# Forty modulation sums go from the expert stage to the first mixer branch, and ScalarE weighs the column one-hots of the gate stage

## The chip, the core and the metric

The kernel runs on one core of a Trainium2 chip. The metric is the device time of one execution in microseconds; less is better. The engines of the core are named as in the profile: PE (TensorE, the matmuls), PEld (its weight loads), DVE (VectorE), ACT (ScalarE), POOL (GpSimd) and SP (SyncE, which here only issues DMAs).

## The reference, cut to what matters

Two transformer-like blocks run one after the other on 512 tokens of width 1024. The first ends in a product-key expert layer ("PEER"), and this is where most of the change lies:

```python
def peer(h, wq, k1, k2, u, v):
    q = (tok @ wq).reshape(-1, PEER_HEADS, 2, PEER_SUB_DIM)
    s1 = einsum("nhd,kd->nhk", q[:, :, 0], k1); s2 = einsum("nhd,kd->nhk", q[:, :, 1], k2)
    v1, i1 = top_k(s1, 16); v2, i2 = top_k(s2, 16)
    cand = v1[..., :, None] + v2[..., None, :]
    top_s, top_c = top_k(cand, 16)               # 16 experts for each of 8 heads
    expert = i1[top_c // 16] * 128 + i2[top_c % 16]
    gate = softmax(top_s)
    act = gelu(einsum("pd,ped->pe", x, u[expert]))
    out = einsum("pe,ped->pd", gate * act, v[expert])
```

Every token picks 128 of 16384 experts. The second block needs modulation values, `silu(c) @ w + b`: each column is a sum over 1024 products. They depend on the input `c` alone, so they can be computed at any time before the second block.

## The kernel before

The program is a row of phases: front, the first mixer branch (`hgrn`, eight heads), the second branch (`gla`, four heads), `mix_out`, `peer`, an attention layer, a dense layer, a scan layer and a last dense layer. Every large product is done as three matmuls of fp32r parts: ACT copies a weight tile of 128x1024 into its high part (`high`), POOL or DVE subtracts that from the tile to get the low part, and PE multiplies.

In `peer`, 384 tokens are computed densely. PE multiplies them with all 128 tiles of `u` (an "up" tile, `up(n)`, 24 matmuls); ACT applies Gelu, and the result is stored to memory (`acts`). Afterwards PE multiplies with all 128 tiles of `v` (the expert stage, last part). What a token gives to an expert is weighted by its gate, which is zero for experts that it did not pick. The table of gates is built on PE in the gate stage: 48 groups of eight tokens, `gate(g)`. For a group DVE writes two sets of one-hots, the rows (which first key, `h` in the profile's names, because they lie in that memory) and the columns (which second key, `peer_cols`), and the columns are multiplied with the gate value. PE multiplies columns by rows for each of the eight tokens, and ACT copies the result from PSUM into `peer_slab`, in two pieces. Rows and columns have two buffers each, so DVE can be two groups ahead.

The order of the work is written out by hand. Each of three blocks has sixteen groups. After a group comes one up tile, except where `g % 5 == 4`: after groups 4, 9 and 14 the next group follows at once. After the sixteen groups come `TAILS` of 7, 8 and 3 up tiles. On ACT a group is `gate(g)` (two copies) and then `up(n)` (Gelu, then `high` of the tile two places on). After the first and the second block ACT also starts the stores of the table to memory.

The other 128 tokens (`FEW`) are handled one expert slot at a time on DVE: POOL fetches the picked rows of `u` with an indirect DMA (`fetch(e)`, eight slots), and DVE multiplies and sums a row of 1024 (`few`, L2049). 128 such row products must be done before the Gelu of these tokens. `MID` and `END` say how many stand in a head of the routing (the top-16 searches of DVE, before the gate stage), `few_after` and `TAIL_FEW` how many stand in the gate stage.

The routing ends when DVE has normalized the gates (L2101). PE then transposes them (L1829), does one more up tile and starts the groups.

The modulation sums are `M.dot` (L192): a DVE instruction over 128x1024 with an accumulated sum. 40 of them stand in the last part of `peer`, with a POOL queue that loads their tiles of 512 KB; the remaining 56 stand in a later dense phase. There `M.rows` is `silu(c)`, computed by ACT and POOL at the start of that part.

## Time and profile before

| | |
|---|---|
| median of three runs | 3612.22 us (3612.14 to 3612.56) |
| profiled execution | 3614.4 us, of which the span from first to last instruction is 3612.7 us |
| mean granted PE clock | 0.975 of full speed |
| PE busy | 3392.0 us (94%) |
| DVE busy | 2415.6 us (67%) |
| ACT busy | 1494.8 us (41%) |
| POOL busy | 1116.7 us (31%) |
| DMA | 604.52 MB |

PE works nearly all the time, so a change moves the end where it removes or adds a wait of PE, or a stretch at a lower PE clock. The busy time of the other engines matters only where PE waits for them. The profile counts each fp32 matmul of the gate products twice (sixteen for a group of eight tokens).

### The profile page before, as it was taken

Reading aid. Unit: us, or ns where it says so; the run is one execution under the profiler, and the core shown is the slowest. Engines: PE = TensorE matmul, PEld = TensorE weight load, DVE = VectorE, ACT = ScalarE, POOL = GpSimd, SP = SyncE. Lnnn points to the kernel's source line nnn. Section 1 sums busy time; section 2 is a strip of 40 time slices with the busy share of each in tenths; the row PEclk is TensorE's granted clock in tenths of the full one; section 3 lists DMA queues with packets and bytes.
Section 4 is the critical chain, followed back from the end, with each engine's and each line's share of the span. In section 5 each row is a group of like instructions: output and inputs, shape, how many; then the busy total and the mean of one; then the engine's idle time right before and its main releaser. Section 6 shows DMA issues by size and latency. Waiting matters only on the chain. (4 is left out here: it accounts for less than half of the span.)

```text
span 3612.7 us, 46897 instructions
## 1 busy us (share of the span) xinstructions
PE 3392.0 (94%) x17929; PEld 2997.4 (83%) x17929; DVE 2415.6 (67%) x4185; ACT 1494.8 (41%) x2094; POOL 1116.7 (31%) x741
## 2 busy tenths in 40 slices
PE   7999989979989999899999999989899998799998
PEld 6888867768879999789999999977688877678886
DVE  6555534435637799978679999766588776755354
ACT  5555545435443333445433333355432234343222
POOL 1222212207326777566543333110200025220002
PEclk9999999989999999899999999999999999899999
DMA  5111111116526777688799999830276522223331
GB/s 189 56 50 57 40 41 47 41 37 228 179 95 190 232 245 257 207 348 296 263 341 373 372 375 376 301 102 18 69 239 223 176 80 58 57 76 100 99 98 61
DMA packets 229823, 604.52 MB, mean 167 GB/s; under 512 B 27840, under 2 KB 102848, under 8 KB 228192
## 3 DMA queue, kind: packets, MB, share of 16 engines
q1 hardware_dynamic: 179696, 409.42, 34.3%
q0 software_dynamic: 47552, 173.04, 12.9%
q10 hardware_dynamic: 2352, 19.07, 1.3%
q8 instruction: 143, 2.34, 0.3%
q14 instruction: 80, 0.66, 0.1%
HBM read 550.31 MB, written 46.14 MB: 165 GB/s over the span
## 5 line engine op out<-in xcount | busy, mean ns | idle before, releaser
L1398 PE MATMUL peer_banks<-peer_h_parts,peer_w_parts 128*128 128x384 f32 (+1 forms) x3456 | 653.0, 348 | 31.6 <-POOL peer_w_parts L1709 26.5
L1398 PEld LDWEIGHTS peer_banks<-peer_h_parts,peer_w_parts 128*128 128x128 f32 x3456 | 611.8, 191 | 58.6 <-POOL peer_w_parts L1709 35.4
L1398 PE MATMUL peer_banks<-peer_act_parts,peer_w_parts 128*128 128x384 f32 x3072 | 535.4, 335 | 4.1 <-DVE peer_w_parts L2153 2.1
L1398 PEld LDWEIGHTS peer_banks<-peer_act_parts,peer_w_parts 128*128 128x128 f32 x3072 | 533.7, 188 | 5.0 <-DVE peer_w_parts L2153 4.7
L1398 PE MATMUL ffn_ps<-h_parts,ffn_w_parts 128*128 128x512 f32 x1920 | 441.0, 392 | 18.2 <-DVE h_parts L2837 11.0
L1398 PEld LDWEIGHTS ffn_ps<-h_parts,ffn_w_parts 128*128 128x128 f32 x1920 | 362.8, 189 | 94.9 <-DVE ffn_w_parts L2647 15.5
L1398 PE MATMUL ffn_ps<-ffn_hidden,ffn_w_parts 128*128 128x512 f32 x1920 | 438.1, 390 | 1.5 <-DVE ffn_hidden L2744 1.5
L1709 POOL TENSOR_TENSOR peer_w_parts<-slots,peer_w_parts 128x1024 fp32r<-128x1024 f32 x142 | 347.9, 2451 | 263.7 <-ACT peer_w_parts L1882 263.4
L1398 PEld LDWEIGHTS ffn_ps<-ffn_hidden,ffn_w_parts 128*128 128x128 f32 x1920 | 360.3, 188 | 77.7 <-issue 3.1
L1882 ACT ACTIVATE peer_w_parts<-slots 128x1024 fp32r<-128x1024 f32 x272 | 287.2, 1056 | 327.5 <-PE peer_banks L1398 311.5
L2492 ACT ACTIVATE ffn_w_parts<-slots 128x1024 fp32r<-128x1024 f32 x160 | 168.6, 1056 | 325.2 <-PE ffn_ps L1398 276.9
L2647 DVE TENSOR_TENSOR ffn_w_parts<-slots,ffn_w_parts 128x1024 fp32r<-128x1024 f32 x160 | 197.7, 1239 | 128.0 <-ACT ffn_w_parts L2492 127.7
L1398 PE MATMUL heads_proj_ps<-h_parts,hgrn_w_parts 128*128 128x512 f32 x960 | 269.4, 413 | 9.2 <-DVE hgrn_w_parts L1054 8.6
L1896 ACT ACTIVATE h<-peer_banks 128x384 f32<-128x384 f32 x128 | 63.0, 492 | 393.8 <-PE peer_banks L1398 380.5
L2153 DVE TENSOR_TENSOR peer_w_parts<-slots,peer_w_parts 128x1024 fp32r<-128x1024 f32 x128 | 156.5, 1223 | 67.3 <-ACT peer_w_parts L1882 67.2
L1398 PEld LDWEIGHTS heads_proj_ps<-h_parts,hgrn_w_parts 128*128 128x128 f32 x960 | 168.2, 190 | 39.9 <-DVE hgrn_w_parts L1054 8.7
L528 POOL TENSOR_TENSOR hgrn_w_parts<-x,hgrn_w_parts 128x1024 fp32r<-128x1024 f32 x38 | 96.2, 2532 | 291.0 <-ACT hgrn_w_parts L764 291.0
L1398 PE MATMUL heads_proj_ps<-h_parts,gla_w_parts 128*128 128x512 f32 x576 | 168.1, 430 | 8.9 <-POOL gla_w_parts L528 5.1
L1398 PEld LDWEIGHTS heads_proj_ps<-h_parts,gla_w_parts 128*128 128x128 f32 x576 | 108.6, 199 | 33.3 <-POOL gla_w_parts L528 7.7
L1322 DVE TENSOR_TENSOR mix_out_w_parts<-out_slots,mix_out_w_parts 128x1024 fp32r<-128x1024 f32 x40 | 80.3, 2007 | 81.0 <-ACT mix_out_w_parts L1257 80.8
L2527 ACT ACTIVATE ffn_buf<-ffn_ps,vec 128x512 f32<-128x512 f32 x64 | 43.9, 688 | 204.9 <-PE ffn_ps L1398 196.9
L2434 POOL TENSOR_TENSOR ffn_gain<-vec,ops 128x8 f32<-128x8 f32 x3 | 0.6, 202 | 409.9 <-DVEq L2675 247.6
(596 smaller groups left out, 5883.9 us busy)
## 6 DMA issues: line engine op xcount, KB each, us to landing
slots<-in_peer_u SPq DMA_DIRECT2D x128, 512.0 KB, 3.9
slots<-in_peer_v SPq DMA_DIRECT2D x128, 512.0 KB, 6.7
slots<-in_mlp_w SPq DMA_DIRECT2D x128, 512.0 KB, 3.5
slots<-in_w_mod SPq DMA_DIRECT2D x56, 512.0 KB, 4.6
peer_acts<-h SPq DMA_DIRECT2D x128, 192.0 KB, 4.2
h<-peer_acts SPq DMA_DIRECT2D x128, 192.0 KB, 7.3
x<-in_w_hg SPq DMA_DIRECT2D x40, 512.0 KB, 3.5
peer_h_parts_memory<-in_w_mod POOLq DMA_DIRECT2D x40, 512.0 KB, 6.0
```

The lines of the kernel that those rows point to most:

```text
L528: nc.gpsimd.tensor_tensor(wp[:, m % 2, 1, :], ring[m % R], wp[:, m % 2, 0, :].bitcast(F32), ALU.subtract).then_inc(w_lo, 1)
L1322: V.tensor_tensor(wp[:, n % 4, 1, :], raw[:, n % R, :], wp[:, n % 4, 0, :].bitcast(F32), ALU.subtract).then_inc(w_lo, 1)
L1398: last = nc.tensor.matmul(out, w(a, k), x(b, k), start=start and k == ks[0] and n == 0, stop=stop and k == ks[-1] and n == 2)
L1709: nc.gpsimd.tensor_tensor(wp[:, p % 2, 1, :], ring.raw[:, p % R, :], wp[:, p % 2, 0, :].bitcast(F32), ALU.subtract).then_inc(w_lo, 1)
L1882: A(wp[:, p % 2, 0, :], ring.raw[:, p % R, :], ACT.Copy).then_inc(w_hi, 1)
L1896: A(stage[:, n % 4, :], a_ps[:, n % 2 * T + FEW:(n % 2 + 1) * T], ACT.Gelu).then_inc(gelu_done, 1)
L2153: V.tensor_tensor(wp[:, p % 2, 1, :], ring.raw[:, p % R, :], wp[:, p % 2, 0, :].bitcast(F32), ALU.subtract).then_inc(v_lo, 1)
L2434: st.do(G.tensor_tensor(gain[:, j, :], gains[j][0], K.ops[:, s, 0:8], ALU.mult))
L2492: A(wp[:, m % 4, 0, :], raw[:, q % R, :], ACT.Copy).then_inc(w_hi, 1)
L2527: A(buf[:, i % 2, :], bank(n), ACT.Relu, bias=K.vec[:, b1 + h * HT + i:b1 + h * HT + i + 1]).then_inc(act_read, 1)
L2647: V.tensor_tensor(wp[:, m % 4, 1, :], raw[:, place(m) % R, :], wp[:, m % 4, 0, :].bitcast(F32), ALU.subtract).then_inc(w_lo, 1)
```

## The change

It has three parts. The 40 modulation sums are computed in the `hgrn` branch, five for each head of the loop, between the steps of DVE. Their tiles are loaded by SP, between the weight tiles of the branch, into two slots of a ring. In the gate stage the columns are written as plain one-hots by one DVE instruction for eight tokens instead of eight instructions, and ACT multiplies them by the gate values (`weigh_ones`, eight instructions, for group g+1 after the copies of group g). And 13 of the 128 row products go from the routing into the gate stage, with new places for the fetches.

```diff
@@ heads_phase, SyncE
+            def mod_tiles(asked, end):
+                for q in range(asked, end):
+                    if q >= MOD_SLOTS:
+                        sp.wait_ge(M.multiplied, q - MOD_SLOTS + 1)
+                    elif q == MOD_SLOTS - 1:
+                        sp.wait_ge(M.silu, 1)
+                    sp.dma_start(early_ring[:, q % MOD_SLOTS, :], d["w_mod"][48 + q]).then_inc(M.ready[q % MOD_SLOTS], 16)
+                return end
...
+                if hg and m == NW + 2:
+                    asked = mod_tiles(asked, 2)
+                if hg and m >= 2 * NW - 1 and m % NW in (NW - 1, 0, 1):
+                    asked = mod_tiles(asked, asked + (1 if m % NW == 1 else 2))
@@ heads_phase, GpSimd
+                if hg and m == NW:
+                    M.start_mul(g, nc.gpsimd)
@@ heads_phase, ScalarE
+                    if H == 0:
+                        M.start_act(act)
@@ heads_phase, VectorE
+                if hg and h is not None:
+                    mod_sums(MODS_HEAD * h, 2)
                 if g is not None:
                     finish(g)
...
+                    if h is not None:
+                        mod_sums(MODS_HEAD * h + 2, 2)
                     if H is not None:
                         forget(H, 0)
                     if h is not None:
                         gates(h)
                         states(h, 0)
+                        mod_sums(MODS_HEAD * h + 4, 1)
@@ peer
-        MID, END = 4, 5
+        MID, END = 3, 4
...
             if tt < 2:
-                return 1 + g % 2
+                return 2
...
-        TAIL_FEW = (9, 9, 3)
+        TAIL_FEW = (8, 7, 3)
...
-            routed = [28 + (e - SLOTS) * 10 // 9 for e in range(SLOTS, ROUTED + SLOTS)]
-            late = [x + 2 for x in late_places()]
+            late = late_places()
+            routed = [min(28 + (e - SLOTS) * 10 // 7, QU + AHEAD if e < ROUTED else late[e - ROUTED] - 2) for e in range(SLOTS, ROUTED + SLOTS)]
+            late = [x + 1 for x in late]
@@ peer, GpSimd, last part
-            g.wait_ge(used, FRONT)
-            for s in range(MG):
-                g.dma_start(M.ring[:, s, :], d["w_mod"][48 + s]).then_inc(M.ready[s], 16)
-            M.start_mul(g, nc.gpsimd)
...
@@ peer, ScalarE
+            def weigh_ones(g):
+                b, first = g % 2, g * G
+                act.wait_ge(ones_done, g + 1)
+                for t in range(G):
+                    last = A(cols[:, b, t, :], cols[:, b, t, :], ACT.Copy, scale=selt[:, 2, first + t:first + t + 1])
+                last.then_inc(cols_done, 1)
...
             up(n)
             up(n + 1)
             n += 2
+            weigh_ones(0)
             for tt in range(BLOCKS):
                 for g in range(groups):
                     gate(tt * groups + g)
+                    if g + 1 < groups:
+                        weigh_ones(tt * groups + g + 1)
...
+                    if tt < BLOCKS - 1 and j == 2:
+                        weigh_ones((tt + 1) * groups)
                     up(n)
@@ peer, VectorE
-                for t in range(G):
-                    one = slice(first + t, first + t + 1)
-                    last = V.tensor_scalar(cols[:, b, t, :], iota_ps, selt[:, 1, one], selt[:, 2, one], ALU.is_equal, ALU.mult)
-                last.then_inc(cols_done, 1)
+                V.tensor_tensor(cols[:, b], iota_ps.unsqueeze(1).to_broadcast([P, G, NKEY]),
+                                selt[:, 1, first:first + G].unsqueeze(2).to_broadcast([P, G, NKEY]), ALU.is_equal).then_inc(ones_done, 1)
...
-                if sums_beside(n):
-                    M.dot(dve, m)
-                    m += 1
```

Where the change puts instructions is seen best in the order in which they stand on an engine. On ACT, from group 3 to group 5 of the first block, this stands before (`peer_slab` are the two copies of a group, `h` is the Gelu of an up tile, `peer_w_parts` its `high`):

```order
L1912 ACTIVATE peer_slab<-peer_banks 128x4x128 x2
L1896 ACTIVATE h<-peer_banks 128x384
L1882 ACTIVATE peer_w_parts<-slots 128x1024
L1912 ACTIVATE peer_slab<-peer_banks 128x4x128 x4
L1896 ACTIVATE h<-peer_banks 128x384
L1882 ACTIVATE peer_w_parts<-slots 128x1024
```

And this stands there after the change:

```order
L1935 ACTIVATE peer_slab<-peer_banks 128x4x128 x2
L1925 ACTIVATE peer_cols<-peer_cols,peer_selt 128x128 x8
L1912 ACTIVATE h<-peer_banks 128x384
L1898 ACTIVATE peer_w_parts<-slots 128x1024
L1935 ACTIVATE peer_slab<-peer_banks 128x4x128 x2
L1925 ACTIVATE peer_cols<-peer_cols,peer_selt 128x128 x8
L1935 ACTIVATE peer_slab<-peer_banks 128x4x128 x2
L1925 ACTIVATE peer_cols<-peer_cols,peer_selt 128x128 x8
L1912 ACTIVATE h<-peer_banks 128x384
L1898 ACTIVATE peer_w_parts<-slots 128x1024
```

The four copies of groups 4 and 5, which stood in a row, now have the eight weighings of group 5 between them.

On PE the same place reads, after the change as before it but for the line numbers:

```order
L1820 MATMUL peer_banks<-peer_cols,h 128x128 x8
L1441 MATMUL peer_banks<-peer_h_parts,peer_w_parts 128x384 x24
L1820 MATMUL peer_banks<-peer_cols,h 128x128 x16
L1441 MATMUL peer_banks<-peer_h_parts,peer_w_parts 128x384 x24
L1820 MATMUL peer_banks<-peer_cols,h 128x128 x8
```

The sixteen matmuls in the middle are groups 4 and 5. Nothing moved here; the second eight of the sixteen now wait for ACT's weighing of group 5.

On DVE, at the start of a head of the `hgrn` loop, this stands before (`hgrn_osq` is `finish`, `hgrn_score` is `mask`, `hgrn_log_gate` is `forget`, `hgrn_state` is `states`):

```order
L1005 TENSOR_TENSOR hgrn_e_q<-hgrn_e_q,hgrn_q 128x512
L1038 SCALAR_TENSOR_TENSOR hgrn_osq<-hgrn_o_ps,vec,hgrn_rstd 128x512
L1042 TENSOR_TENSOR h<-hgrn_osq,hgrn_sgate 128x512
L1010 TENSOR_TENSOR hgrn_q_dec<-hgrn_q_dec,hgrn_q 128x1024
L1014 COPY_PREDICATED hgrn_score<-triu,hgrn_score_ps 128x512
L949 TENSOR_SCALAR hgrn_log_gate<-hgrn_log_gate,oml,lb 128x768
```

And this after it:

```order
L192 SCALAR_TENSOR_TENSOR hgrn_mod_ring,modv<-hgrn_mod_ring,hgrn_c_rows 128x1024 x2
L1072 SCALAR_TENSOR_TENSOR hgrn_osq<-hgrn_o_ps,vec,hgrn_rstd 128x512
L1076 TENSOR_TENSOR h<-hgrn_osq,hgrn_sgate 128x512
L1044 TENSOR_TENSOR hgrn_q_dec<-hgrn_q_dec,hgrn_q 128x1024
L1048 COPY_PREDICATED hgrn_score<-triu,hgrn_score_ps 128x512
L192 SCALAR_TENSOR_TENSOR hgrn_mod_ring,modv<-hgrn_mod_ring,hgrn_c_rows 128x1024 x2
L983 TENSOR_SCALAR hgrn_log_gate<-hgrn_log_gate,oml,lb 128x768
```

Two sums stand ahead of `finish`, two between `mask` and the first `forget`, and a fifth (not shown) between `states` and the second `forget`.

## Rows read from the trace of the kernel before

**Rows 1.** Busy time by stage: stretch, length, engines, PE clock, DMA share, GB/s.

```profile
1040.00:1470.00 430.00, 406.10 (x2203) 382.29 (x2204) 359.86 (x1020) 146.23 (x202) 285.36 (x149) 0.97 0.69 221
1470.00:1842.00 372.00, 342.41 (x2168) 337.48 (x2166) 284.87 (x598) 177.08 (x215) 223.45 (x152) 0.96 0.77 284
1842.00:2382.00 540.00, 537.54 (x3085) 535.71 (x3086) 465.08 (x707) 199.28 (x265) 151.86 (x146) 1.00 0.96 347
```

**Rows 2.** Waits of PE, 1460 to 1842: total us, times, longest.

```profile
PE peer_banks L1398 <- POOL peer_w_parts L1709: 19.5, 9, 6.9
PE peer_banks L1829 <- DVE peer_sel L2101: 12.1, 1, 12.1
PE peer_banks L1804 <- issue: 8.4, 5, 3.5
```

**Rows 3.** Timeline of PE, first block: start, us, what, idle before.

```profile
1469.40 2.18 PE L1829 MATMUL peer_banks<-ident,peer_sel 128*128 128x128 f32 x9 [12.09 <-DVE peer_sel L2101]
1471.23 5.78 PE L1398 MATMUL peer_banks<-peer_h_parts,peer_w_parts 128*128 128x384 f32 x24
1476.85 1.95 PE L1804 MATMUL peer_banks<-peer_cols,h 128*128 128x128 f32 x16
...
1496.39 4.41 PE L1398 MATMUL peer_banks<-peer_h_parts,peer_w_parts 128*128 128x384 f32 x24
1504.34 3.21 PE L1804 MATMUL peer_banks<-peer_cols,h 128*128 128x128 f32 x16 [3.54 <-issue]
...
1518.41 1.95 PE L1804 MATMUL peer_banks<-peer_cols,h 128*128 128x128 f32 x16
```

**Rows 4.** Timeline of all engines around groups 9 and 10.

```profile
1536.25 3.82 PE L1804 MATMUL peer_banks<-peer_cols,h 128*128 128x128 f32 x32
1536.45 0.49 ACT L1896 ACTIVATE h<-peer_banks 128x384 f32<-128x384 f32 x1 [2.54 <-PE peer_banks L1398]
1536.84 1.05 ACT L1882 ACTIVATE peer_w_parts<-slots 128x1024 fp32r<-128x1024 f32 x1
...
1537.78 3.82 ACT L1912 ACTIVATE peer_slab<-peer_banks 128x512 f32<-128x512 f32 x4
...
1539.56 2.63 DVE L2119 TENSOR_SCALAR peer_cols<-peer_banks,peer_selt 128x128 f32<-128x128 f32 x8
...
1539.83 4.41 PE L1398 MATMUL peer_banks<-peer_h_parts,peer_w_parts 128*128 128x384 f32 x24
```

**Rows 5.** ACT with operands for each partition: ns min/median/max, first and last start.

```profile
L2569 ACT ACTIVATE x<-x,ffn_alpha_g x8: 706/707/709, 2542.9 to 2547.2; 128x512 f32<-128x512 f32 x8
L1926 ACT ACTIVATE peer_slab<-h,modv,gs_ffn x8: 477/478/480, 1053.1 to 1055.8; 128x128 f32<-128x128 f32 x8
```

**Rows 6.** ACT with constants alone, by form: busy us, mean ns, idle before.

```profile
L2571 ACT ACTIVATE x<-x 128x512 f32<-128x512 f32 x8 | 5.0, 622 | 0.0
L3196 ACT ACTIVATE mla_probt<-mla_banks 128x128 f32<-128x128 f32 x8 | 2.2, 271 | 0.0
```

**Rows 7.** Stretches as in group 1, for clock and DMA share.

```profile
2542.80:2546.00 3.20, 3.20 (x9) 2.46 (x9) 1.85 (x2) 3.20 (x7) 0.00 (x0) 0.50 0.83 227
1062.00:1068.00 6.00, 5.80 (x18) 5.80 (x19) 0.00 (x0) 0.45 (x1) 2.47 (x2) 0.50 0.54 165
1567.40:1611.90 44.50, 35.62 (x185) 34.17 (x184) 20.42 (x40) 10.40 (x14) 28.01 (x19) 0.88 1.01 411
```

**Rows 8.** Timeline of PE after an idle time elsewhere.

```profile
2542.44 8.92 PE L1398 MATMUL ffn_ps<-h_parts,ffn_w_parts 128*128 128x512 f32 x31 [4.24 <-DVE ffn_w_parts L2647]
```

**Rows 9.** Timeline of DVE in one `hgrn` head.

```profile
259.82 0.75 DVE L1038 SCALAR_TENSOR_TENSOR hgrn_osq<-hgrn_o_ps,vec,hgrn_rstd 128x512 f32<-128x512 f32 x1 [9.54 <-ACT hgrn_rstd L836]
...
268.92 0.68 DVE L949 TENSOR_SCALAR hgrn_log_gate<-hgrn_log_gate,oml,lb 128x768 f32<-128x768 f32 x1 [5.31 <-ACT hgrn_log_gate L774]
...
277.15 0.68 DVE L949 TENSOR_SCALAR hgrn_log_gate<-hgrn_log_gate,oml,lb 128x768 f32<-128x768 f32 x1 [2.82 <-ACT hgrn_log_gate L774]
```

**Rows 10.** DMA issues, 100 to 450: count, KB each, median us to landing.

```profile
x<-in_w_hg SPq DMA_DIRECT2D x30, 512.0 KB, 3.5
```

**Rows 11.** Waits of PE, 1840 to 1860.

```profile
PE peer_banks L1398 <- DVE peer_act_parts L2148: 2.0, 1, 2.0
```

**Rows 12.** Timeline of DVE in the routing of the third head.

```profile
1193.04 1.22 DVE L2049 SCALAR_TENSOR_TENSOR peer_few_rows<-peer_few_rows,peer_banks 128x1024 f32<-128x1024 f32 x1 [17.68 <-DMA peer_few_rows<-in_peer_u_rows,peer_few_idx]
```

More of the change, by code:

```diff
@@ L472, in heads_phase @@
         pg = K.heads_ps
+        if hg:
+            ph.sb("mod_gap", [P, 1280])
+            early_ring = ph.sb("mod_ring", [P, MOD_SLOTS, D])
+            M = Modulation(nc, K, ph, d, 48, PEER_MODS, MOD_SLOTS, [(2, 48)], ring=early_ring,
+                           prod=early_ring[:, MOD_SLOTS - 1:MOD_SLOTS, :])
+            silu_kept = ph.sems("silu_kept")
         ptr = ph.banks("trans_ps", 2)
@@ L508, in _ @@
         def _(sp):
+            def mod_tiles(asked, end):
[6 more added lines that the diff above has]
+                return end
+            asked = 0
             for m in range(R if hg else 2, heads * NW):
@@ L512, in _ @@
                 sp.dma_start(ring[m % R], w_dram[m]).then_inc(ready[m % R], 16)
+                if hg and m == R:
+                    sp.dma_start(M.rows[:, 0, :], d["c_rows"][2].partition_broadcast(P)).then_inc(M.rows_in, 16)
+                if hg and m == NW + 2:
+                    asked = mod_tiles(asked, 2)
+                if hg and m >= 2 * NW - 1 and m % NW in (NW - 1, 0, 1):
+                    asked = mod_tiles(asked, asked + (1 if m % NW == 1 else 2))
             if nxt is not None:
@@ L520, in _ @@
                     sp.dma_start(nxt.ring[:, m, :], d["w_gla"][m]).then_inc(nxt.ready[m], 16)
+            if hg:
+                mod_tiles(asked, PEER_MODS)
+                sp.dma_start(K.silu_row, M.rows[0:1, 0, :]).then_inc(silu_kept, 16)
         @block.gpsimd
@@ L534, in _ @@
                                             ALU.subtract).then_inc(nxt.w_lo, 1)
+            if hg:
+                M.finish(g, nc.gpsimd, M.multiplied)
+                g.wait_ge(silu_kept, 16)
         @block.tensor
@@ L890, in _ @@
                         forget(H, 1)
+                    if H == 0:
+                        M.start_act(act)
+                    if H is not None:
                         log_forget(H, 0)
@@ L1065, in _, with mod_sums @@
                     V.tensor_tensor(dst[:, 1, k, :], src[:, k, :], dst[:, 0, k, :].bitcast(F32), ALU.subtract).then_inc(h_lo, 1)
+            def mod_sums(first, count):
+                for q in range(first, first + count):
+                    M.dot(dve, q)
             st.then(V.memset(score[:], 0.0))
@@ L1427 @@
 OUT_BLOCKS = BLOCKS - 1
-PEER_MODS = 40
+PEER_MODS, MOD_SLOTS = 40, 2
+MODS_HEAD = PEER_MODS // 8
 FFN_MODS = 4 * 24 - PEER_MODS
@@ L1482, in peer @@
     with Phase(nc, "peer") as ph:
-        hp_space = ph.sb("h_parts_memory", [P, 2 * KT * T])
+        ph.sb("h_parts_memory", [P, 2 * KT * T])
         wp = ph.sb("w_parts", [P, 2, 2, KT * P], F32R)
@@ L1496, in peer @@
             gate_in_sb = alias.enter_context(nc.sbuf_tensor("peer_gate_in", [P, 4, OUT_BLOCKS, PT], F32))
-            mod_rows = alias.enter_context(nc.sbuf_tensor("peer_mod_rows", [P, 1, D], F32))
         cols = ph.sb("cols", [P, 2, G, NKEY])
@@ L1543, in peer @@
         act_in_sb = rows_flat.rearrange("p b x -> p (b x)")[:, 0:4 * DENSE].rearrange("p (s t) -> p s t", s=4)
-        MG = 4
-        mod_ring = hp_space[:, 0:MG * D].rearrange("p (s t) -> p s t", s=MG)
-        mod_prod = hp_space[:, MG * D:(MG + 1) * D].rearrange("p (s t) -> p s t", s=1)
-        M = Modulation(nc, K, ph, d, 48, PEER_MODS, MG, [(2, 48)],
-                       ring=mod_ring, rows=mod_rows, prod=mod_prod)
         banks = ph.banks("banks", 8)
@@ L1574, in peer @@
         x_done, sq_done, paired, sum_done, root = ph.sems("x_done", "sq_done", "squares_paired", "sum_done", "root")
+        ones_done = ph.sems("ones_done")
         few_x_done, few_x_turned, few_idx_done, few_dotted, few_act_done, few_added, iota_stored, x_out, x_back = ph.sems(
@@ L1577, in peer @@
         few_in = ph.sems(*[f"few_in{i}" for i in range(SLOTS)])
-        silu_kept = ph.sems("silu_kept")
         stored = ph.sems(*[f"act_stored{i}" for i in range(4)])
@@ L1631, in peer @@
         assert early_fetches == list(range(IN_FRONT)) and IN_FRONT >= CALLS
-        def sums_beside(n):
-            return n % 3 == 1 and n // 3 <= M.tiles
         def adds_beside(n):
@@ L1717, in _ @@
                 f += 1
-            g.wait_ge(g_done, 2 * BLOCKS * groups)
-            g.dma_start(M.rows[:, 0, :], d["c_rows"][2].partition_broadcast(P)).then_inc(M.rows_in, 16)
-            g.wait_ge(used, FRONT)
-            for s in range(MG):
-                g.dma_start(M.ring[:, s, :], d["w_mod"][48 + s]).then_inc(M.ready[s], 16)
-            M.start_mul(g, nc.gpsimd)
-            g.dma_start(K.silu_row, M.rows[0:1, 0, :]).then_inc(silu_kept, 16)
-            m, c = 0, BEFORE
-            for n in range(1, V_TILES):
-                if sums_beside(n):
-                    if m + MG < M.tiles:
-                        g.wait_ge(M.multiplied, m + 1)
-                        g.dma_start(M.ring[:, m % MG, :], d["w_mod"][48 + m + MG]).then_inc(M.ready[m % MG], 16)
-                    m += 1
-                if adds_beside(n):
-                    if c + SLOTS < CALLS:
-                        fetch(CALLS + c + SLOTS)
-                    c += 1
-            M.finish(g, nc.gpsimd, M.multiplied)
-            g.wait_ge(silu_kept, 16)
+            while f < 2 * CALLS:
+                fetch(f)
+                f += 1
             for k in (0, 2, 4):
@@ L2161, in _ @@
             few(1)
-            m = 0
             for n in range(2, V_TILES):
@@ L2166, in _ @@
                 act_low(n)
-                if sums_beside(n):
-                    M.dot(dve, m)
-                    m += 1
                 if adds_beside(n):
                     few(1)
-            assert done[0] == 2 * CALLS and m == M.tiles
+            assert done[0] == 2 * CALLS
             dve.wait_ge(x_back, 16)
@@ L2177, in _ @@
                                        in1=K.x[:, k, :], op0=ALU.mult, op1=ALU.add).then_inc(x_done, 1)
-            dve.wait_ge(M.v, 1)
             st.do(V.tensor_scalar(K.ops[:, 0, :], K.mod[:, 56:72], 1.0, None, ALU.add))
```

2 lines of the change are left out of this document (removed).

## The prediction

> **What bounds the kernel now.** I read the busy time by stage first [rows 1]. In the last stage (the `v` tiles) PE is busy 537.5 of 540 us at full clock: PE bounds it, and DVE's 465 us lie beside it. In the routing PE is busy 406 of 430 us, in the gate stage 342 of 372 us at a mean clock of 0.96. So something is to be won in the gate stage, and nearly nothing in the last one, though DVE and POOL carry most of the moved work there.
>
> The waits of PE name the losses of the gate stage [rows 2]: 19.5 us for low parts of up tiles, 12.1 us for the end of the routing (`peer_sel`), and 8.4 us in five pieces for one-hots. The timeline shows the second and third [rows 3]. After its idle 12.1 us PE takes 2.18 us for nine transposes and 5.78 us for an up tile that takes 4.41 elsewhere. Group 4 starts at 1504.34, 3.54 us late, and its matmuls take 3.21 instead of 1.95 us.
>
> The 19.5 us are something else. They lie at the ends of the first and second block, where the table is stored. From 1567.4 to 1611.9 the DMA share is 1.01 and PE is busy 35.6 of 44.5 us [rows 7]. The data set the pace there, and neither DVE nor ACT. The change removes none of those data: 8 and 7 row products stand in the tails instead of 9 and 9, but by the new places nearly as many rows are fetched during them. I leave this stall as it is.
>
> **The rhythm of a group.** Measured from the start of its matmuls, in group 9 [rows 4]: Gelu at 0.20, `high` at 0.59, first copy at 1.53. Four copies take 3.82 us, so two take 1.95 us and end at about 3.5. PE needs 1.84 us for a group (1.95 with its last drain) and about 4.1 for the up tile, together 5.94: between groups 0 and 4 each start follows the last by that much, as 1476.85 and three more such steps plus the up tile at 1496.39 show [rows 3]. ACT is thus done with group g well ahead of PE's next group.
>
> **Price of one weighing.** No row has this form (128x128, in SBUF, one scale per partition). With 512 elements the same operation takes 707 ns, and with constants alone 622 ns [rows 5, 6]: the operand costs 85 ns. With 128 elements and two such operands it takes 478 ns and starts every 0.386 us (2.7 us over seven steps) [rows 5]; constants alone, out of PSUM, 271 ns [rows 6]. One operand fewer than 478 gives about 390 ns, and a start every 0.30 us. Eight take 7 x 0.30 + 0.39 = 2.45 us. Bounds: 1.5 us if it costs what the plain copy does, 3.2 us if it costs what the form with two operands does. I take 2.45.
>
> The row gives 85 ns for an operand. The Trainium skill (ScalarE: Activation LUTs, "What ACT_TABLE_LOAD costs") gives 93 ns for each and lets instructions that follow one another overlap by as much; by its figures a weighing is 386 ns and eight take an estimated 2.44 us. The sum would not change by it.
>
> **Part 1, weighing where an up tile follows (36 groups and the start of each block).** The copies end at 3.5, the weighing at 6.0, and PE may start the next group at 6.1 instead of 5.94. ACT then runs a cycle of 0.39 + 0.94 + 1.95 + 2.4 = 5.7 us, under 5.94, so this delay doesn't grow: cost 0. At 0.386 us each it would be 6.4 to 6.5 us, and some 0.5 us would come with each of the 36 groups: +18 us, kept for the range.
>
> **Part 2, weighing where no up tile follows.** Groups 4, 9 and 14 of each block are followed at once by the next one. Before, DVE had written both, and PE ran 32 matmuls in 3.82 us [rows 4]. Now ACT's order is copies of group 9, weighing of 10, copies of 10, and PE can't start group 10 before the weighing: copies end at 3.5, weighing at 6.0, start at 6.1. It could start at 1.84. That is 4.25 us of idle PE, nine times: +38.3 us. Behind the waiting matmuls stand the up tile and all after it. Nothing lies beside it, since PE has no other work in its queue. With 1.5 us for the weighing it is 3.3 us each, with 3.2 us 5.0.
>
> **Part 3, the first group.** `weigh_ones(0)` stands behind the Gelu and `high` of the up tile before group 0. PE ends that tile at about 1477.0 [rows 3]; 0.39 + 0.94 + 2.45 + 0.1 later the columns are ready: +4.1 us. The first groups of blocks 1 and 2 are weighed in the tail, where ACT is idle between tiles: 0.
>
> **Part 4, the clock.** Idle stretches of this size are followed by the lower clock. After 4.24 us of idle PE elsewhere [rows 8] the granted clock is 0.50 for 3.2 us [rows 7], and another stretch shows 0.50 for 6 us with PE busy [rows 7]. Half clock for 3.2 to 6 us costs 1.6 to 3 us of work; I take 1.75. Ten stalls pay it, less the last pairs of blocks 0 and 1, whose loss disappears in the tails that wait for data anyway: 8 x 1.75 = +14 us.
>
> The rows show this drop of the clock, from full speed to half (2.4 to 1.2 GHz). The Trainium skill (TensorE: Matmul & The Clock Gate, "HAM oscillation — how this bites in real kernels") says the same of idle gaps between bursts of matmuls, and speaks against this change. By it all ten stalls pay, which is +17.5 us in place of +14.
>
> **Part 5, what DVE gains.** Eight column instructions took 2.63 us [rows 4]; one of 128x1024 is like the rows' (1.22 us by the row product's length in [rows 12], same size). Each group gains some 1.4 us, and gives up 1.1 for half a row product more in blocks 0 and 1. This is worth something only where PE waits for DVE. First: 13 products fewer in the routing, each 1.22 us, are 15.9 us, more than the 12.1 us of waiting. PE's wait for `peer_sel` goes, with its clock (0.9 us on the transposes, 1.4 on the up tile): −14.4 us. What is late next is nothing: DVE also waited 17.7 us for a row at 1193 [rows 12]; with MID 3 that row is asked for later in DVE's order. Second, the loss at groups 4 and 5 of block 0: group 6 starts at 1518.41; from 1496.39 on, undisturbed, it would be 4.24 + 1.84 + 5.94 us later, at 1508.4. −10.0 us. Third, the three small waits for one-hots (8.4 − 3.5 − 2.4): −2.5 us. Fourth, small waits in the routing itself: of the 24 idle us [rows 1] about 3 stand between its heads; −2 us, bounds 0 and 4.
>
> **Part 6, sums out of the last stage.** 40 instructions of 1.2 us leave DVE, 21 MB leave POOL's queue. PE is not waiting there, so: 0. Only at its start, where POOL's loads and its product stood in the way, PE waited 2.0 us for DVE [rows 11]: −2 us.
>
> **Part 7, sums into the `hgrn` branch.** Each head gets five, 6 us of DVE. It idles 9.5 us before `finish`, 5.3 us before the first `forget` and 2.8 us before the second [rows 9]. Two, two and one sums fit there. Two slots mean that the first pair must be read before the second is asked for; a load of that size takes 3.5 us [rows 10], and 9 us lie between `finish` and the first `forget`. SP's waits for `multiplied` stand ahead of weight tiles, and those tiles are then issued late by what the wait lasts; 30 of them in 350 us [rows 10] are one every 11.7 us, and each lands in 3.5, so a wait of a few us is absorbed. Cost 0; if all sums lay on the path it would be 8 x 6 = 48 us, which the idle rows speak against.
>
> **Sum.** +38.3 + 4.1 + 14 − 14.4 − 10.0 − 2.5 − 2 − 2 = +25.5 us. Against the profiled execution (3614.4 us, its span 3612.7) that is 3640; that execution stands 2.2 us above the median of 3612.2, so I predict **3637 us**.
>
> **The rivals.**
>
> The stalls come, the clock stays (6%). Not every wait lowers it: the last stage has one of 2.0 us [rows 11] and a mean clock of 1.00 [rows 1]. Then +14 falls away: 3624 us. Against it: the 3.5 us before group 4 lowered it [rows 3].
>
> ACT becomes the bound in every group (10%). At 0.386 us a weighing, parts 1 and 2 give +18 and +7: 3662 us. For it: nothing measured has exactly this form.
>
> The weighing is hidden (10%; the other side). If ACT has the columns of groups 5, 10 and 15 before PE has finished the group ahead, only the gains are left: 3612.2 − 30.9 = 3581 us. It decides at 1.84 us after a group's start; the copies alone end at 3.5, and the order of ACT has them first. So it needs a stall that something else makes shorter. A milder form, 1.5 us for a weighing, gives 3.3 us a stall and 3628 with the clock's loss, 3614 without (4% in it, no change).
>
> The sums in `hgrn` cost (4%). A dot that waits for its tile ahead of `mask` would hold up PE: 1 to 2 us for each head, 3650.
>
> The gate stage doesn't change (4%): a wait for data takes over everything that is won or lost, about 3612.
>
> **How the numbers follow.** The forecast holds 62%: 3625 to 3652. About 0.2% (7 us) is what a measurement can tell from no change. Slower takes the forecast, the kept clock, the bound on ACT and the `hgrn` case: 82%. Same: 8%. Faster: 10%. The range leaves out the hidden weighing and the far end of the ACT case: 3612 to 3664.
>
> **What would show it.** In the profile after: three stalls of PE per block before a group's matmuls, each of 4 to 5 us, put down to ACT `peer_cols`, followed by a granted clock of 0.50; eight weighings in 2.4 to 2.5 us; no wait for `peer_sel`; the last stage again 537 us; `hgrn` as long as before. Wrong it would be if the weighings overlapped with the copies, or if PE's clock stayed up.

## The result and the profile after

The changed kernel takes 3633.93 us (median of four runs, 3631.97 to 3636.2), against 3612.38 before. The ratio is 1.0058, with a 95% interval from 1.0045 to 1.0070: it is slower by some 21 us, 0.6%, clear of no change by its interval. 3637 was predicted. The profiled execution took 3633.33 us, its span 3631.6, 18.9 us more than the one of before. One execution of a later run, that with the sums alone, took 3824.93 us in a slower state of the chip and is left out of its ratio.

First the waits of PE from 1430 to 1880 us of the changed kernel (us in total, times, longest), to be laid beside [rows 2]:

```profile
PE peer_banks L1820 <- issue: 34.2, 9, 3.8
PE peer_banks L1441 <- POOL peer_w_parts L1744: 11.4, 6, 5.3
PE peer_banks L1820 <- ACT peer_cols L1925: 4.0, 1, 4.0
PE peer_banks L1441 <- DVE peer_w_parts L2177: 1.3, 1, 1.3
PE peer_banks L1845 <- DVE peer_sel L2127: 1.0, 1, 1.0
```

The wait for `peer_sel` fell from 12.1 to 1.0 us, and the five pieces for one-hots (8.4 us) are gone. In place of the latter stand nine waits of 3.8 us and one of 4.0. The wait for low parts also fell, from 19.5 to 11.4 us, though nothing of the change touches it.

The nine are put down to "issue", so their cause has to be read from the timeline. Here are all engines at groups 8 to 10 of the first block (start us, us, instruction, idle before):

```profile
1515.59 1.95 PE L1820 MATMUL peer_banks<-peer_cols,h 128*128 128x128 f32 x16
...
1518.71 1.21 DVE L2143 TENSOR_TENSOR peer_cols<-peer_banks,peer_selt 128x1024 f32<-128x1024 f32 x1
...
1521.56 1.95 PE L1820 MATMUL peer_banks<-peer_cols,h 128*128 128x128 f32 x16
1521.76 0.49 ACT L1912 ACTIVATE h<-peer_banks 128x384 f32<-128x384 f32 x1 [0.41 <-PE peer_banks L1441]
...
1522.15 1.05 ACT L1898 ACTIVATE peer_w_parts<-slots 128x1024 fp32r<-128x1024 f32 x1
...
1523.09 1.93 ACT L1935 ACTIVATE peer_slab<-peer_banks 128x512 f32<-128x512 f32 x2
...
1524.81 2.40 ACT L1925 ACTIVATE peer_cols<-peer_cols,peer_selt 128x128 f32<-128x128 f32 x8
...
1527.32 3.52 PE L1820 MATMUL peer_banks<-peer_cols,h 128*128 128x128 f32 x16 [3.81 <-issue]
```

Group 9 starts at 1521.56. ACT goes through the Gelu, `high`, two copies and the eight weighings of group 10, which end at 1527.21. PE starts group 10 at 1527.32, 0.11 us later. The one-hots that ACT weighs were ready long before: DVE had written them by 1519.92. From group 8 to group 9 the distance is 5.97 us (before it was 5.94 to 5.95), although ACT weighs there too.

Next the stretches (length, busy us of PE, PEld, DVE, ACT and POOL, PE clock, DMA share, GB/s): the gate stage, the last stage, some 3 us behind each of three waits, and the up tiles at the end of the first block, where the data set the pace:

```profile
1470.00:1860.00 390.00, 344.46 (x2104) 339.52 (x2103) 218.63 (x268) 275.30 (x579) 224.12 (x153) 0.93 0.77 279
1860.00:2400.00 540.00, 538.67 (x3097) 535.87 (x3096) 423.16 (x631) 194.42 (x266) 113.75 (x105) 1.00 0.90 308
...
1527.40:1530.60 3.20, 3.20 (x17) 3.20 (x17) 0.78 (x2) 1.04 (x1) 2.45 (x3) 0.52 1.01 360
1558.60:1561.90 3.30, 3.30 (x17) 3.30 (x17) 0.00 (x0) 1.05 (x1) 2.40 (x3) 0.50 1.03 395
1777.50:1780.70 3.20, 3.19 (x15) 3.20 (x16) 0.00 (x0) 1.05 (x1) 0.00 (x0) 0.50 0.38 154
...
1561.90:1603.00 41.10, 36.14 (x188) 34.86 (x188) 14.12 (x22) 13.82 (x23) 23.63 (x15) 0.93 1.02 411
```

Against [rows 1] the stretch that begins at 1470 is 18 us longer, at a clock of 0.93 for 0.96. The stage itself grew by more, since it now begins earlier: from the transposes to the first matmul of the last stage it is 407.4 us (1455.42 to 1862.81) in place of 373.0 (1469.40 to 1842.39). DVE's busy time in the stretch fell from 285 to 219 us, and PE waits for that engine only 1.0 us at the transposes and 1.3 us at the start of the last stage. In the last stage DVE has 42 us less to do, and PE's busy time is the same. Behind the waits the clock is about half: 0.50 to 0.64 in the 3.2 us behind each of the ten. The group at 1527.32 takes 3.52 us for 1.95. At 1777.50 the DMA share is only 0.38 and the clock is 0.50 all the same.

### The profile page after: what moved, and what is told of

Its sections match the earlier page's. It is cut to its first block and busy times, and to the rows that moved or that the text cites. A ratio compares the mean times of both kernels' runs of the same rounds, so it can differ in the third digit from the quotient of the medians.

```text
span 3631.6 us, 46946 instructions
## 1 busy us (share of the span) xinstructions
PE 3403.6 (94%) x17929; PEld 3009.5 (83%) x17929; DVE 2344.7 (65%) x3849; ACT 1596.3 (44%) x2477; POOL 1075.4 (30%) x699
## 3 DMA queue, kind: packets, MB, share of 16 engines
q0 software_dynamic: 41616, 151.54, 11.5%
## 5 line engine op out<-in xcount | busy, mean ns | idle before, releaser
L1441 PE MATMUL ffn_ps<-h_parts,ffn_w_parts 128*128 128x512 f32 x1920 | 441.0, 392 | 18.6 <-DVE h_parts L2856 11.4
L1441 PEld LDWEIGHTS ffn_ps<-h_parts,ffn_w_parts 128*128 128x128 f32 x1920 | 362.9, 189 | 95.4 <-DVE ffn_w_parts L2666 16.1
L1820 PE MATMUL peer_banks<-peer_cols,h 128*128 128x128 f32 x768 | 108.7, 302 | 38.2 <-issue 34.2
L1820 PEld LDWEIGHTS peer_banks<-peer_cols,h 128*128 128x128 f32 x768 | 104.2, 216 | 40.8 <-issue 39.9
```

Source lines behind the costliest of these rows:

```text
L1441: last = nc.tensor.matmul(out, w(a, k), x(b, k), start=start and k == ks[0] and n == 0, stop=stop and k == ks[-1] and n == 2)
L1820: last = nc.tensor.matmul(g_bank(n)[:, i * P:(i + 1) * P], rows[:, b, t, :], cols[:, b, t, :], start=True, stop=True)
```

## Experiments

Each kernel differs from the changed one by the edit shown. Ratios are to the kernel before in the same session (its medians there were 3610.3 to 3611.7 us, its single runs 3606 to 3619), so differences of two or three us between medians carry nothing. A recorded ratio is not the quotient of the two medians and can differ from it by 0.1%. Two theories were open. The first says that the loss lies in ACT's order in the pairs of groups, as a wait and the clock behind it. The second says that the pairs take up a slack which another wait (data, DVE) would fill.

### DVE weighs the second group of each pair

```diff
+        def on_dve(g):
+            return g % groups % 5 == 0 and g % groups > 0
...
+                if on_dve(g):
+                    for t in range(G):
+                        one = slice(first + t, first + t + 1)
+                        last = V.tensor_scalar(cols[:, b, t, :], iota_ps, selt[:, 1, one], selt[:, 2, one], ALU.is_equal, ALU.mult)
+                    last.then_inc(cols_dve, 1)
+                    return
```

> The changed kernel, but in the nine groups that follow another one directly (5, 10 and 15 of each block) DVE writes the weighted columns in eight instructions, as the kernel before did; ACT weighs the other 39. Theory A (the loss is ACT's order in these pairs): the nine waits of PE of 3.8 us go, 34.2 us, and with them the low clock behind each, some 1.7 us each. Of this a part comes back in the tails, which wait for data, up to 8 us, and DVE has 1.4 us more work in five groups, which makes 26.6 us of it against PE's 25.6: up to 6 us. So 3590 us, 3580 to 3600. Theory B (the pairs only take up a slack that another wait would fill at once, the low parts or DVE): under 15 us are won, 3620 us or more.

Measured: 3590.39 us, ratio 0.9936 (0.9919 to 0.9952). The waits of PE in that kernel, 1430 to 1880:

```profile
PE peer_banks L1441 <- POOL peer_w_parts L1750: 15.6, 8, 4.8
PE peer_banks L1826 <- ACT peer_cols L1933: 3.9, 1, 3.9
```

The nine waits are gone and 43.5 us with them, of which 34.2 are the waits themselves. The wait for low parts rose by 4.2 us: the tails (the up tiles that stand behind the sixteen groups of a block) took part of it back. The first theory holds. Moving nine of 48 weighings turns a loss of 0.6% into a gain of 0.6%.

### ACT weighs ahead of the copies in a pair

```diff
+                    if g % 5 == 4:
+                        weigh_ones(tt * groups + g + 1)
                     gate(tt * groups + g)
-                    if g + 1 < groups:
+                    if g + 1 < groups and g % 5 != 4:
                         weigh_ones(tt * groups + g + 1)
```

> The changed kernel, but where the next group follows directly, ACT weighs its columns ahead of the two copies of the group, not behind. Measured from the start of the first group of the pair the weighing then ends at 1.5 + 2.4 = 3.95 and not at 5.7 us, so PE waits 2.1 us in place of 3.8. Theory A (wait and clock as before, only shorter): 9 x 1.7 = 15 us less, 3618 us. Theory B (a wait of 2.1 us does not lower the clock): 15 us more are saved, 3604 us. Theory C (the copies, now late, hold up the groups behind): little changes, 3630 us.

Measured: 3616.93 us, ratio 1.0012 (1.0002 to 1.0021). The timeline at the first pair:

```profile
1486.83 1.22 DVE L2143 TENSOR_TENSOR h<-peer_banks,peer_selt 128x1024 f32<-128x1024 f32 x1 [1.32 <-PE peer_banks L1820]
...
1490.81 1.95 PE L1820 MATMUL peer_banks<-peer_cols,h 128*128 128x128 f32 x16
...
1492.34 2.43 ACT L1925 ACTIVATE peer_cols<-peer_cols,peer_selt 128x128 f32<-128x128 f32 x8
...
1494.68 3.83 ACT L1935 ACTIVATE peer_slab<-peer_banks 128x512 f32<-128x512 f32 x4
1494.88 2.06 PE L1820 MATMUL peer_banks<-peer_cols,h 128*128 128x128 f32 x16 [2.12 <-DVE h L2143]
```

The wait fell to 2.12 us, as worked out, and the time by 17 us, where the first theory said 15 without a gain of clock. The rows show a mixture for the clock. These are the stretches behind the first, second and seventh of the nine waits of 2.12 us:

```profile
1494.90:1498.10 3.20, 3.20 (x24) 3.20 (x25) 3.20 (x6) 3.20 (x4) 2.46 (x3) 1.00 0.86 291
1522.90:1526.10 3.20, 3.20 (x19) 3.20 (x20) 3.10 (x6) 3.19 (x4) 2.45 (x4) 0.71 0.88 302
1766.70:1769.90 3.20, 3.20 (x15) 3.20 (x16) 1.52 (x2) 2.73 (x3) 0.00 (x0) 0.50 0.43 169
```

Behind four of the nine it stayed at 1.00, behind the other five it was 0.50 to 0.73. The wait for low parts rose from 11.4 to 18.7 us, so the tails took back about as much as the clock can have given. The timeline puts the wait of PE down to DVE's rows; DVE had written those of this group by 1488.05, and ACT's weighing ended at 1494.77, 0.11 us before PE started. The name of a releaser is wrong here.

### ACT weighs both groups ahead of the pair

```diff
+                    if g % 5 == 3:
+                        weigh_ones(tt * groups + g + 2)
```

(and no weighing behind the group with `g % 5 == 4`)

> The changed kernel, but ACT weighs the columns of both groups of a pair ahead of the up tile before the pair. The 5.7 us of waits of a pair become some 0.5 us ahead of the first or second group and 1.6 us ahead of the group after the pair, since ACT has 26.4 us of work in five groups against PE's 25.6. Theory A (only waits of 2 us and more lower the clock): 3634 - 15 - 14 = 3605 us, with a granted clock of 1.0 in the pairs. Theory B (every wait lowers it): 3618 us.

Measured: 3603.21 us, ratio 0.9974 (0.9963 to 0.9984). The timeline of PE at the first pair:

```profile
1490.30 1.95 PE L1820 MATMUL peer_banks<-peer_cols,h 128*128 128x128 f32 x16
1492.55 1.13 PE L1820 MATMUL peer_banks<-peer_cols,h 128*128 128x128 f32 x8 [0.30 <-issue]
1494.75 1.16 PE L1820 MATMUL peer_banks<-peer_cols,h 128*128 128x128 f32 x8 [1.07 <-ACT peer_slab L1935]
```

One wait of 3.8 us has become 0.3 and 1.1 us, and PE stays at full speed (each half group takes 1.13 to 1.16 us in all nine pairs). The second wait is not the one that I had worked out: the weighing of both groups ended at 1492.45, and PE goes on when ACT's first copy out of PSUM ends, at about 1494.7. It waits for a bank whose copy is late, not for weighed columns. The low parts are at 18.2 us here. The time is the expected one.

### PE kept busy during the waits

```diff
+                if filled(g):
+                    if g:
+                        pe.wait_ge(g_stored, 2 * g - 2)
+                    for _ in range(28):
+                        nc.tensor.transpose(g_bank(2 * g)[:, 0:P], K.ident[:], K.ident[:])
                 pe.wait_ge(rows_done, g + 1)
```

> The changed kernel with 28 further transposes of the identity on PE (some 3.3 us) in each of the ten waits for ACT, into a bank that the group overwrites afterwards. They change no other engine's work. Theory A (the slow groups behind the waits are the clock): the groups start when they did, but at full clock, and 1.7 us are saved at each of ten, some less in the tails: 3619 us, 3616 to 3624, with a granted clock of 1.0 behind the waits. Theory B (the groups behind the waits are slow because of memory or PSUM): 3634 us.

Measured: 3622.39 us, ratio 1.0025 (1.0014 to 1.0037). PE at the second pair, and then the stretch behind the wait (columns as above):

```profile
1518.43 1.95 PE L1828 MATMUL peer_banks<-peer_cols,h 128*128 128x128 f32 x16
1520.21 3.22 PE L1819 MATMUL peer_banks<-ident 128*128 128x128 f32 x28
1524.30 2.02 PE L1828 MATMUL peer_banks<-peer_cols,h 128*128 128x128 f32 x16 [0.87 <-ACT peer_cols L1933]
```

```profile
1524.30:1527.50 3.20, 3.20 (x24) 3.20 (x25) 1.89 (x3) 2.04 (x3) 2.43 (x3) 1.00 0.97 369
```

From group 9 to group 10 it is 5.87 us here and 5.76 in the changed kernel, so the stall is the same. But group 10 takes 2.02 us in place of 3.52, at a clock of 1.00 and with the same busy memory. The same holds behind all ten waits (clock 1.00, 2.02 us), so the slow groups are the clock's work and not that of memory. The low clock cost 11.5 us of time in the medians. In the two traces the three blocks of groups, each from its first group's start to its last group's end, take 273.9 us with the filling and 291.1 without: 17.2 us for ten waits. The two tails take 93.0 us with it and 88.9 without, so 4.1 of the 17.2 are given back there. The Trainium skill (TensorE: Matmul & The Clock Gate, "HAM oscillation — how this bites in real kernels") describes this, half rate after idle gaps between bursts; the traces agree, 0.52 without the filling and 1.00 with it.

### More work on ACT

```diff
-                    last = A(cols[:, b, t, :], cols[:, b, t, :], ACT.Copy, scale=selt[:, 2, first + t:first + t + 1])
+                    for c in (slice(0, P // 2), slice(P // 2, P)):
+                        last = A(cols[:, b, t, c], cols[:, b, t, c], ACT.Copy, scale=selt[:, 2, first + t:first + t + 1])
```

> The changed kernel with each weighing cut into two halves of 64 columns, 16 instructions a group for 8: some 3.7 us for 2.4. It prices the slack of ACT. Theory A (ACT has 0.4 us of slack in a group with an up tile, 5.5 of 5.95 us): 0.9 us come in each of 36 groups and 1.4 us in each of nine pairs, 3680 us, 3665 to 3690. Theory B (the slack is larger, only pairs lengthen): 3646 us.

Measured: 3681.33 us, ratio 1.0189 (1.0172 to 1.0206). The waits for columns, and then the timeline of ACT in one group:

```profile
PE peer_banks L1820 <- issue: 64.1, 39, 5.0
```

```profile
1521.19 3.88 ACT L1926 ACTIVATE peer_cols<-peer_cols,peer_selt 128x64 f32<-128x64 f32 x16
...
1528.16 3.89 ACT L1926 ACTIVATE peer_cols<-peer_cols,peer_selt 128x64 f32<-128x64 f32 x16
```

There are 39 waits in place of nine, and ACT is not idle in the stretch around these rows: it is now the bound in ordinary groups too, 39 of the 45 steps from one group to the next. Its weighing takes 3.88 us for 2.41, 1.47 more, and groups follow each other by 6.97 us for 5.97, 1.00 more. So the slack of ACT in a group of the changed kernel is 0.47 us, near the 0.4 of theory A. The prediction's rival in which ACT bounds every group was that close: a weighing needed to last only 0.06 us longer.

### The other parts of the change

DVE weighs all 48 groups; sums and products stay moved:

```diff
+        def on_dve(g):
+            return True
```

> The changed kernel with all columns weighed by DVE as before: the sums and the 13 products stay moved. Theory A (DVE can't hold the products and the weighing together): rows 1.2, columns 2.6 and two row products 2.6 us are 6.4 us for each group against PE's 5.94, and over five groups 32 against 25.6, so DVE becomes the bound in the first two blocks: some 35 us come back of the 54 that the waits for ACT cost, 3610 to 3630 us, with PE waiting for one-hots in most groups. Theory B (DVE's gain was never needed, the moved weighing only costs): the time falls to about 3585 us.

Measured: 3601.91 us, ratio 0.9973 (0.9962 to 0.9985), better than theory A's range. The waits, and then a stretch of the first block:

```profile
PE peer_banks L1826 <- issue: 18.3, 7, 3.9
PE peer_banks L1441 <- POOL peer_w_parts L1750: 14.4, 9, 5.3
```

```profile
1492.40:1552.00 59.60, 53.27 (x352) 52.66 (x353) 59.60 (x131) 30.90 (x36) 37.98 (x29) 0.97 0.81 274
```

DVE is busy 59.60 of 59.60 us: it is the bound there, as theory A has it. But PE waits only 18.3 us for it, in seven pieces, each before the second group of a pair. The expectation had DVE's work too large. I had added durations, 6.4 us a group, but each instruction starts before the one ahead of it has ended: the rows of three groups in a row start at 1464.61, 1470.57 and 1476.53, 5.96 us apart. Five groups are 29.8 us of DVE against 25.6 of PE, not 32. I had also forgotten that DVE begins a block up to two groups ahead. In the changed kernel it is busy 219 us of the gate stage, so weighing on ACT does buy room there; it was bought at a place where it costs more.

The 13 products back in the routing, with the old places of fetches:

```diff
-        MID, END = 3, 4
+        MID, END = 4, 5
...
-                return 2
+                return 1 + g % 2
...
-        TAIL_FEW = (8, 7, 3)
+        TAIL_FEW = (9, 9, 3)
```

> The changed kernel with the 13 row products back in the routing and the old places of fetches (sums and weighing stay moved). Theory A: PE waits some 12 us for the end of the routing again, and has the lower clock behind it (2.3 us): 3646 us, 3640 to 3652. Theory B (lighter DVE in the gate stage gives it back, or the first weighing lies in that wait): no more than 3 us slower than the changed kernel, 3634 to 3637.

Measured: 3657.55 us, ratio 1.0121 (1.0103 to 1.0139), 23.6 us slower than the changed kernel where 12 were expected. PE at groups 4 and 5, and DVE ahead of them:

```profile
1510.77 2.02 PE L1819 MATMUL peer_banks<-peer_cols,h 128*128 128x128 f32 x16 [3.41 <-issue]
1517.86 3.75 PE L1819 MATMUL peer_banks<-peer_cols,h 128*128 128x128 f32 x16 [5.07 <-issue]
```

```profile
1504.69 1.23 DVE L2074 SCALAR_TENSOR_TENSOR peer_few_rows<-peer_few_rows,peer_banks 128x1024 f32<-128x1024 f32 x1 [5.16 <-DMA peer_few_rows<-in_peer_u_rows,peer_few_idx]
...
1511.79 1.22 DVE L2074 SCALAR_TENSOR_TENSOR peer_few_rows<-peer_few_rows,peer_banks 128x1024 f32<-128x1024 f32 x1 [3.60 <-DMA peer_few_rows<-in_peer_u_rows,peer_few_idx]
```

Beside the 12.1 us for `peer_sel` the loss at groups 4 and 5 is back, though DVE's columns are cheap here. Its cause is neither the weighing nor DVE's load: DVE stands idle for picked rows of `u` that have not landed, 17.5 us in the first block, and the one-hots of the next groups stand behind these products in its order. The kernel before has the same wait, though no row above shows it:

```profile
1499.33 1.22 DVE L2049 SCALAR_TENSOR_TENSOR peer_few_rows<-peer_few_rows,peer_banks 128x1024 f32<-128x1024 f32 x1 [6.12 <-DMA peer_few_rows<-in_peer_u_rows,peer_few_idx]
```

In the changed kernel DVE doesn't wait for a row in the first block. This run puts back the products and the places of the fetches together, so which of the two brings the rows in time isn't shown. In the traces group 0 starts 16.9 us later than in the changed kernel and the first block is 6.0 us longer. The 24.4 us of the prediction (14.4 and 10.0) are near the 23.6 measured, but not term by term. My expectation for this run had left out the first block.

Only the sums moved:

```diff
+        def on_dve(g):
+            return True
...
+        MID, END = 4, 5
+        TAIL_FEW = (9, 9, 3)
```

> Only the 40 sums are moved; weighing and products as in the kernel before. Theory A: the first mixer branch hides the sums; at the start of the last stage the two waits of 2.1 and 2.0 us shrink, with the low clock behind: 3608 us, 3605 to 3611. Theory B (the sums cost in the branch, 1 to 2 us a head): 3616 us or more.

Measured: 3610.73 us beside 3610.34, ratio 0.9997 (0.9988 to 1.0007). No change; 0 to 4 us were expected to be won. The start of the last stage:

```profile
1841.32 28.84 PE L1441 MATMUL peer_banks<-peer_act_parts,peer_w_parts 128*128 128x384 f32 x156 [2.09 <-DVE peer_w_parts L2190]
```

The wait of 2.0 us [rows 11] is gone, and the last stage is 2.3 us shorter in the trace (535.1 for 537.4), but a win of that size is below what the times can tell.

DVE weighs only the very first group (`return g == 0`):

> The changed kernel with only the very first group's columns weighed by DVE, the other 47 by ACT. Theory A: PE's wait of 4.0 us before group 0 goes, less up to 0.7 for DVE's longer work there, and 1.7 us of low clock with it: 3634 - 5 = 3629 us. Theory B (what PE gains there it loses at group 5, whose one-hots come later): 3634 us.

Measured: 3631.11 us, ratio 1.0057 (1.0041 to 1.0072), 2.8 us less than the changed kernel and not outside the runs' spread. The wait of 4.0 us became one of 0.7 for DVE before group 0, and one of 0.8 for ACT before group 1, which now has to be weighed at once.

Both mends together, DVE for the first group and the second of each pair:

```diff
+        def on_dve(g):
+            return g == 0 or g % groups % 5 == 0 and g % groups > 0
```

> Both mends together: DVE weighs groups 5, 10 and 15 of each block and the very first, ACT the other 38. Theory A (independent terms): 3590.4 - 5 = 3585 us, 3582 to 3589. Theory B (DVE, with ten groups of its own, becomes late in the first block): 3590 us.

Measured: 3584.77 us (3580.21 to 3588.42), ratio 0.9926 (0.9912 to 0.9939). It beats the kernel before and the changed one. The gain over the mend of the pairs alone (ratio 0.9936) isn't clear of noise, since the intervals overlap. Its waits of PE in the gate stage:

```profile
PE peer_banks L1441 <- POOL peer_w_parts L1750: 19.4, 8, 6.2
PE peer_banks L1826 <- ACT peer_cols L1933: 0.8, 1, 0.8
PE peer_banks L1826 <- DVE peer_cols L2154: 0.7, 1, 0.7
```

What is left are mainly the low parts, 19.4 us, as much as in the kernel before.

## Why the prediction was right

**Price of a weighing (2.45 us for eight).** Eight took 2.40 to 2.41 us. One took 392 ns (median of 384), where 390 was worked out from the rows. The estimate from the Trainium skill (ScalarE: Activation LUTs, "What ACT_TABLE_LOAD costs") was 386 ns, and the trace agrees within 6 ns.

**Part 1 (no cost where an up tile follows).** Right: from group 8 to 9 it is 5.97 us. The slack is 0.47 us, by the run with halves.

**Part 2 (nine waits of 4.25 us, +38.3).** Right in mechanism, place and count; each was 3.8 us, +34.2 together, where the signs asked for 4 to 5 us. The copies of a group take 1.72 us up to the first weighing (1523.09 to 1524.81), and I had put them down with 1.95, whose last part is the drain. Another 0.11 us is the drain of PE's own last matmul, which the rows count as busy (1.95 for 1.84). The profile calls these waits "issue" and not ACT `peer_cols`, as the signs had it.

**Part 3 (+4.1).** The wait was 4.0 us. What a mend wins is less, since the next group then waits 0.8 us.

**Part 4 (the clock, +14).** Shown by the filled waits: 17.2 us in the three blocks, of which the tails give back 4.1. The prediction had 17.5 for ten waits and set 3.5 aside for the tails.

**Part 5 (−14.4 and −10.0, −2.5, −2).** The timeline of PE after the routing in the changed kernel:

```profile
1455.42 1.20 PE L1845 MATMUL peer_banks<-ident,peer_sel 128*128 128x128 f32 x9 [1.02 <-DVE peer_sel L2127]
1456.37 4.42 PE L1441 MATMUL peer_banks<-peer_h_parts,peer_w_parts 128*128 128x384 f32 x24
1464.74 2.98 PE L1820 MATMUL peer_banks<-peer_cols,h 128*128 128x128 f32 x16 [3.95 <-ACT peer_cols L1925]
```

The transposes come 14.0 us earlier, 1455.42 for 1469.40 [rows 3], they and the up tile are at full clock, and group 0 starts 12.1 us earlier in spite of its wait of 4.0: 16.1 us won, where 16.4 were put down. Of these, 1.8 us lie ahead of `peer` (its first matmul starts at 1043.02 for 1044.78) and are not this part's. The 8.4 us for one-hots are gone. Against a block without any wait (79.0 us, the last one in the run with both mends) the kernel before lost 12.8 us in its three blocks, where 10.0 and 2.5 were put down. But the term of 10.0 was put under what DVE gains in a group. What stood behind it was DVE's wait for fetched rows, which the run without the moved products brings back. A slip without effect on the sum: half a row product is 0.6 us and not 1.1.

**The low parts ("I leave this stall as it is").** This was right about the cause, the data: ahead of POOL's low parts ACT waits for DMAs in the first tail, 12.8 us before and 10.5 after. It was wrong in leaving the stall at its size. The waits fell by 8.1 us at the same DMA share (1.02 for 1.01 in the first tail), and rose again in every run that shortened the blocks, to between 12.7 and 19.4. The places of the fetches are not the reason: with the old places back (the run without the moved products) they stay at 11.8. My reading is that in a stretch that the data bound, part of what is lost before it is refunded, and part of what is won is taken. The order of the runs fits only roughly (14.4 us with all columns on DVE, 18.7 with the weighing first, though that kernel is the slower one), so it isn't shown as a rule. I had allowed for 3.5 us of it, in the clock of two pairs; the tails and the last up tiles took 8.6.

**Parts 6 and 7 (0, −2).** The sums lie beside other work. The largest wait of PE in the branch is 8.6 us in both kernels, one of 1.7 us is new, and the first matmul of `peer` comes no later (1.8 us earlier). DVE's idle time before `finish` fell from 9.54 [rows 9] to 6.98 us:

```profile
260.72 0.75 DVE L1072 SCALAR_TENSOR_TENSOR hgrn_osq<-hgrn_o_ps,vec,hgrn_rstd 128x512 f32<-128x512 f32 x1 [6.98 <-ACT hgrn_rstd L867]
```

**The last stage (−2).** From its first matmul to its closing sum it takes 537.4 us before and 533.5 after, in the timelines of PE (before, then after):

```profile
1842.39 10.16 PE L1398 MATMUL peer_banks<-peer_act_parts,peer_w_parts 128*128 128x384 f32 x48 [2.12 <-DVE peer_w_parts L2153]
...
2379.78 4.77 PE L1871 MATMUL peer_banks<-h,ones 128*128 128x512 f32 x10
```

```profile
1862.81 7.52 PE L1441 MATMUL peer_banks<-peer_act_parts,peer_w_parts 128*128 128x384 f32 x42 [1.31 <-DVE peer_w_parts L2177]
...
2396.32 4.74 PE L1887 MATMUL peer_banks<-h,ones 128*128 128x512 f32 x10
```

2.0 us of it are the wait of [rows 11]. The rest lies at its start, where the clock over the first 15.6 us is 0.89 before and 1.00 after. The run with the sums alone has 2.3 us of this in its trace and none in its time.

**The sum.** The timelines of PE in the two profiled executions, 18.9 us apart, can be cut at the same places and laid beside the terms:

| piece of PE's timeline | before | after | change | forecast |
|---|---|---|---|---|
| start to group 0 | 1476.9 | 1464.7 | −12.1 | −12.3 |
| three blocks of groups | 249.9 | 291.1 | +41.2 | +39.8 |
| the two tails | 94.9 | 88.9 | −6.0 | 0 |
| last up tiles | 20.7 | 18.1 | −2.6 | 0 |
| last stage | 537.4 | 533.5 | −3.9 | −2 |
| from its closing sum on | 1232.9 | 1235.3 | +2.4 | 0 |
| all | 3612.7 | 3631.6 | +18.9 | +25.5 |

The forecast column is −14.4, −2 and +4.1 for the first piece and +38.3, +14, −10.0 and −2.5 for the second. So the terms of the change itself came out, together, within 1.6 us. The 6.6 us between +25.5 and +18.9 are what the tails and the last up tiles refunded, and smaller pieces that partly cancel. Between the medians, 21.5 us apart, 24.6 was forecast; that 3637 lies only 3 us above 3633.9 is in part the luck of which executions were profiled. The one before stood 2.2 us above its median, and the one after 0.6 below.

Left open: the 2.4 us from the closing sum on, in phases that the change doesn't touch. In the changed kernel PE does the same number of matmuls there in 1.7 us more of busy time (1141.2 for 1139.5). The run with the sums alone is 2.6 us longer there too. What brings it isn't known, and no run was made for it.

## What to carry to other kernels

Before work goes to an engine with low busy time, go through that engine's own order at the places where the rhythm is broken. ACT had 41% of the span before and 44% after, and ended on time behind every up tile; the loss lay only where two groups follow each other and the copies of the first stand ahead of the columns of the second. Here nine of 48 instances decided the sign of the change, and giving these back to the old engine kept the gain everywhere else.

When waits of PE are added up, add what the lower clock takes behind each, and look for a later stretch that the data bound: it may refund part of it. Here it was 8.6 us.

## What the runs showed of the hardware

Nine waits of PE of 2.12 us in one kernel, at the same place of its rhythm, were followed by the full clock four times and by 0.50 to 0.73 five times. Ten waits of 3.8 to 4.0 us were followed by 0.50 to 0.64, each over 3.2 us. The length alone doesn't decide: in the run without the moved products a wait of 3.41 us was followed by a group at full clock (2.02 us). Two waits of 0.3 and 1.1 us in one pair left it at 1.00. Transposes of an identity, whose result nobody reads, held the clock at 1.00 behind all ten waits.

Halving the columns of an ACT instruction (128x64 for 128x128, one scale for each partition) saves 58 ns of 392 (334 ns). An estimate from these two sizes is that some 276 of the 392 ns don't depend on the number of columns.
